# First expert's rows by 0/1 products, early choice for tiles 0 to 2, weights ordered behind the second expert's rows

## What is computed

```python
def hier_moe(t, w_group, b_group, w_expert, b_expert, w_gate, w_up, w_down):
    g_logits = t @ w_group + b_group              # (512, 4)
    g_w, g_idx = lax.top_k(softmax(g_logits), 1)
    e_logits = (t @ w_expert + b_expert).reshape(T, 4, 4)
    e_sel = take_along_axis(e_logits, g_idx)      # the 4 experts of the group
    e_w, e_idx = lax.top_k(softmax(e_sel), 2)
    ...
    for e in range(16):
        hdn = silu(t @ w_gate[e]) * (t @ w_up[e])
        y = y + combine[:, e:e + 1] * (hdn @ w_down[e])
    return y

h = h + hier_moe(rms_norm(h, m_norm[layer]), ...)
```

## Time and profile before

| | us |
|---|---|
| median of 3 runs (1140.46 to 1142.6) | 1140.63 |
| profiled execution | 1143.3 |
| its span, first to last instruction | 1141.5 |
| PE busy | 1078.8 (95%) |
| DVE busy | 508.6 (45%) |
| ACT busy | 282.6 (25%) |
| POOL busy | 265.0 (23%) |
| 16 DMA engines, mean over the span | 248 GB/s |

### The profile page before, as it was taken

One profiled execution on the slowest core, in us unless ns is written; L12 is line 12 of the kernel. 1 busy time (PEld: TensorE's weight loads), 2 busy tenths in 40 slices (PEclk: granted clock), 3 DMA queues, 4 the chain that ended last, 5 costly groups with the idle time before them and its releaser, 6 DMA issues.

```text
span 1141.5 us, 17926 instructions
## 1 busy us (share of the span) xinstructions
PE 1078.8 (95%) x7469; PEld 647.0 (57%) x7469; DVE 508.6 (45%) x939; ACT 282.6 (25%) x461; POOL 265.0 (23%) x373
## 2 busy tenths in 40 slices
PE   6999999999999999996999999999989999999991
PEld 5688887874444433342788877777844444344430
DVE  3465237545533233326422357763355432343317
ACT  4442344320000000004232227763210000000012
POOL 1200012004333443123000013340023344433131
PEclk9899999999999999998999999999989999999996
DMA  9443311248999999998223210004279999999965
GB/s 322 127 146 112 106 38 74 110 186 331 402 422 421 422 423 423 423 418 288 102 75 111 79 69 1 2 1 166 71 263 415 419 421 421 422 423 423 423 230 198
DMA packets 68699, 283.24 MB, mean 248 GB/s; under 512 B 15048, under 2 KB 15216, under 8 KB 44064
## 3 DMA queue, kind: packets, MB, share of 16 engines
q1 hardware_dynamic: 47440, 239.32, 52.3%
q0 software_dynamic: 15232, 38.69, 9.4%
q10 hardware_dynamic: 5968, 4.40, 1.2%
HBM read 259.96 MB, written 22.41 MB: 247 GB/s over the span
## 4 chain that ended last, share of the span: by engine, by line
PE 81%; DVE 6%; DMA 4%; issue 4%; POOL 4%; ACT 1%; SPq 0%; POOLq 0%; DVEq 0%
PE ps L1843 41%; PE ps L1510 11%; PE ps L1512 10%; PE ps L1511 10%; DMA w_f<-in_m_w_up 2%; POOL xn_r L2295 1%; PE ps L1742 1%; DVE h L1384 1%; DMA xn<-output_table,pos 1%; PE ps L1520 1%; PE ps L1971 1%; DVE xn_r L1435 1%; POOL xn_r L2288 1%; PE ps L1654 1%; PE ps L1732 1%
## 5 line engine op out<-in xcount | busy, mean ns | idle before, releaser
L1843 PE MATMUL ps<-raw,s_f 128*32 128x256 f32 (+1 forms) x1536 | 175.8, 455 | 1.3 <-issue 0.7
L1843 PE MATMUL ps<-w_f,s_f 128*32 128x256 f32 (+1 forms) x1536 | 173.0, 451 | 2.6 <-issue 1.8
L1843 PE MATMUL ps<-xT_f,s_f 128*32 128x256 f32 (+1 forms) x1344 | 150.1, 451 | 0.4 <-DMA xT_f<-in_m_w_up 0.4
L1198 DVE TENSOR_TENSOR pad<-pad,ps 128x256 f32<-128x256 f32 x32 | 13.5, 421 | 296.6 <-ACT pad L790 296.6
L1843 PEld LDWEIGHTS ps<-raw,s_f 128*32 128x32 f32 (+1 forms) x1536 | 67.8, 119 | 103.5 <-issue 84.1
L1843 PEld LDWEIGHTS ps<-w_f,s_f 128*32 128x32 f32 (+1 forms) x1536 | 69.1, 119 | 95.4 <-issue 70.5
L1843 PEld LDWEIGHTS ps<-xT_f,s_f 128*32 128x32 f32 (+1 forms) x1344 | 59.7, 119 | 93.0 <-issue 74.0
L939 DVE SCALAR_TENSOR_TENSOR w_lo<-raw,gainT,w_hi 128x512 fp32r<-128x512 f32 x88 | 60.2, 746 | 105.3 <-ACT w_hi L594 105.3
L1208 DVE STREAM_TRANSPOSE s_f<-pad 32x128 f32<-32x128 f32 x256 | 103.0, 403 | 4.1
L1510 PE MATMUL ps<-w_hi,xT_hi 128*128 128x512 f32 x240 | 97.7, 407 | 5.9 <-DVE w_lo L939 2.9
L2252 POOL DMA_DIRECT2D output_table<-pad x60 | 33.7, 566 | 293.0 <-ACT pad L796 282.5
(11 more groups left out here) (299 smaller groups left out, 1470.8 us busy)
## 6 DMA issues: line engine op xcount, KB each, us to landing
raw<-in_m_w_down SPq DMA_DIRECT2D x28, 1024.0 KB
w_f<-in_m_w_down SPq DMA_DIRECT2D x28, 1024.0 KB
xT_f<-in_m_w_gate SPq DMA_DIRECT2D x26, 1024.0 KB
xT_f<-in_m_w_up SPq DMA_DIRECT2D x26, 1024.0 KB
raw<-in_m_w_gate SPq DMA_DIRECT2D x18, 1024.0 KB
raw<-in_m_w_up SPq DMA_DIRECT2D x18, 1024.0 KB
w_f<-in_m_w_gate SPq DMA_DIRECT2D x18, 1024.0 KB
w_f<-in_m_w_up SPq DMA_DIRECT2D x18, 1024.0 KB
```

What stands on the lines that cost most here:

```text
L1198: ve.tensor_tensor(hid2[:, 0:2 * P], sil2[:, 0:2 * P], ps[:, 0, 2 * P:4 * P], ALU.mult)
L1843: ins = te.matmul(ps[rows * n:rows * (n + 1), bank + kind, 0:width // parts], stationary(k, kind), weights(k, parts, n), start=k == 0, sto ...
```

## The change

Three things are changed, in both layers alike.

1. The choice of experts is split by tiles. `select(0, 3)` and the ranks of tiles 0 to 2 are computed while the last tile's projection still runs; `select(3, 4)` and its ranks follow behind its logits. The ranks now lie in PSUM bank 6.
2. Expert 0's rows are no longer gathered. DVE writes for each token and each of the 96 places a 1 where the token takes that place (`first_sel`, float32), and PE multiplies the rows of `xn`, which are on chip, by these lists: 4 tiles x 8 feature blocks = 32 products `first_rows`, whose sum is expert 0's x, already transposed. Expert 1's list is formed by itself (`second_sel`, with `id_parts`, eight products of one column), and the whole-row gather now serves expert 1. The lists for all experts (`lists`), the quarter numbers and expert 1's transposes now stand inside expert 0's kind 0 and kind 1 products (`behind`). The warming products (`kept_warm`) are gone, and expert 1's rows are no longer gathered by quarters.
3. On the SP queue, pair 4 stands ahead of the wait, and the wait is now for expert 1's rows. Pair 6 waits in addition until the products have read `xn`.

The core of the diff:

```diff
@@ load_pair
                 if p == OWN:
                     sp.wait_ge(A["rows_stored"], 16 * NT * (layer + 1))
+                    sp.wait_ge(E["x_tr"], 4 * layer + 2)
@@ step, on the SP queue
+                    load_down(layer, p + 2, e - 1, g)
                     if isinstance(e, int) and e == 1:
-                        sp.wait_ge(E["x_loaded0"], x_loads(layer, 0, -1))
-                    load_down(layer, p + 2, e - 1, g)
+                        sp.wait_ge(E["x_loaded1"], x_loads(layer, 1, -1))
@@ DVE, out_tiles
+            def places_of(sel, e, first, last):
+
+                return tt(sel[:, first:last, :], index_1[:, :].unsqueeze(1).broadcast_to([P, last - first, CAP]),
+                          rank_of_first[:, first:last, e:e + 1].broadcast_to([P, last - first, CAP]), ALU.is_equal)
+
+            def ranks_in(layer, first, last):
+
+                dve.wait_ge(M["ranks_done"], 2 * layer + (1 if first == 0 else 2))
+                link(stt(rank_of_first[:, first:last, :], ps[:, 6, 0:NT * NE].rearrange("p (i e) -> p i e", e=NE)[:, first:last, 0:2], 1.0,
+                         sel_b[:, first:last, 0:2], ALU.add, ALU.mult))
...
-                logits_in(j - 1)
+                link(logits_in(j - 1))
+                select(0, j)
                 add(j, 1)
+                ranks_in(layer, 0, j)
+                places_of(first_sel, 0, 0, j).then_inc(V["places_ready"], 1)
@@ DVE, router
+                select(last, NT)
+                places_of(second_sel, 1, 0, last)
+                ranks_in(layer, last, NT)
+                places_of(first_sel, 0, last, NT).then_inc(V["places_ready"], 1)
+                places_of(second_sel, 1, last, NT).then_inc(V["places_ready"], 1)
...
+                x_half(layer, 0, 0).then_inc(E["x_in"], 1)
...
+                x_half(layer, 0, 1).then_inc(E["x_in"], 1)
+                dve.wait_ge(M["lists_done"], 4 * layer + 1)
+                ve.tensor_copy(token_now[:, 1:2], ps[0:CAP, 2, 2 * P:2 * P + 1]).then_inc(V["tokens_ready"], 1)
@@ PE, out_proj
                 logits(last, range(BK))
+                ranks(layer, range(last))
                 h_transposed_to(last, range(BK, KT))
+                pe.wait_ge(V["places_ready"], 5 * layer + 1)
+                pe.wait_ge(V["xn_ready"], NT * layer + last)
+                first_rows(EARLY[0:4])
                 logits(last, range(BK, KT))
...
+            def first_rows(products):
+
+                for t, k in products:
+                    at = CAP * (k % 4)
+                    ins = te.matmul(ps[:, 4 + k // 4, at:at + CAP], xn[:, t, every(KT, k)], first_sel[:, t, :],
+                                    start=t == 0 and k % 4 == 0, stop=t == NT - 1, skip_group_check=True)
+                return ins
@@ PE, experts
-                x_transposed(E, layer, x_loads(layer, 0, -1))
-                up(I, 0, 0, 0, layer > 0)
-                lists(2 * layer + 2, 7, MAX_OVER)
+                up(I, 0, 0, 0, layer > 0, (lambda: lists(5 * layer + 4, 7, NE), second_rows))
+                lists(5 * layer + 5, 7, MAX_OVER)
@@ PE, router
-                kept_warm(3)
...
+                first_rows(EARLY[4:18])
+                ranks(layer, range(last, NT))
+                first_rows(EARLY[18:20])
+                pe.wait_ge(V["places_ready"], 5 * layer + 2)
+                pe.wait_ge(A["xn_scaled"], layer + 1)
+                first_rows((last, k) for k in range(4)).then_inc(E["x_tr"], 1)
+                first_rows(EARLY[20:])
+                first_rows((last, k) for k in range(4, KT)).then_inc(E["x_tr"], 1)
+                pe.wait_ge(V["places_ready"], 5 * layer + 3)
+                for t in range(NT):
+                    for c in range(2):
+                        ins = te.matmul(ps[0:CAP, 2, 2 * P:2 * P + 1], second_sel[:, t, :], id_parts[:, c, t:t + 1],
+                                        start=t + c == 0, stop=t + c == NT)
+                ins.then_inc(M["lists_done"], 1)
@@ POOL, experts
-                gather(E, token[:, 0:1])
+                gather(token_now[:, 1:2], E["x_loaded1"])
                 pool.wait_ge(V["quads_ready"], layer + 1)
-                gather_quarters(1)
                 gather_quarters(2)
```

More of the change, by code:

```diff
@@ L217, in trunk @@
         gain_rows = pad[0:5 * KT, 13312:13312 + P]
-        free = [6144]
+        free = [11264]
         def scratch(*shape):
@@ L260, in trunk @@
         index = sb("index", [P, CAP])
+        index_1 = sb("index_1", [P, CAP])
+        id_parts = sb("id_parts", [P, 2, NT], BF16)
         parity = sb("parity", [P, 2])
@@ L1790, in every, with ranks @@
                 return slice(k, k + n * (P - 1) + 1, n)
+            EARLY = [(t, k) for f in (0, 1) for t in range(NT - 1) for k in range(4 * f, 4 * f + 4)]
+            def first_rows(products):
[4 more added lines that the diff above has]
+                return ins
+            def ranks(layer, tiles):
+                pe.wait_ge(V["sel_ready"], 2 * layer + (1 if tiles[0] == 0 else 2))
+                for i in tiles:
+                    o = ps[:, 6, NE * i:NE * (i + 1)]
+                    for j in range(i):
+                        te.matmul(o, ones_b[:, :], sel_b[:, j, :], start=j == 0, stop=False)
+                    ins = te.matmul(o, before[:, :], sel_b[:, i, :], start=i == 0, stop=True)
+                if tiles[-1] == NT - 1:
+                    o = ps[:, 6, NE * NT:NE * (NT + 1)]
+                    for j in range(NT):
+                        ins = te.matmul(o, ones_b[:, :], sel_b[:, j, :], start=j == 0, stop=j == NT - 1)
+                ins.then_inc(M["ranks_done"], 1)
             def x_transposed(S, i, loads):
-                pe.wait_ge(S["x_loaded0"], loads)
+                pe.wait_ge(S["x_loaded1" if S is E else "x_loaded0"], loads)
                 for f in (0, 1):
@@ L1846, in column_tiles, with up @@
                     return ins
-                def up(i, p, m, g=0, reuse=True):
-                    pe.wait_ge(E["x_in"], i + 1)
+                def up(i, p, m, g=0, reuse=True, behind=None):
+                    pe.wait_ge(E["x_in"], x_ins(layer, i) - (behind is not None))
                     if reuse:
@@ L1855, in up @@
                                 pe.wait_ge(*pair_of(layer, p + n, g))
+                                if n and behind is not None:
+                                    pe.wait_ge(E["x_in"], x_ins(layer, i))
                             w = pair_slots[slot_of(p + n)]
@@ L1867, in up @@
                                 ins.then_inc(M["blk_used"], 2)
+                            elif behind is not None:
+                                behind[n]()
                 def down(i, p, m, g=0):
@@ L1966, in last_to_tokens @@
                     ins.then_inc(M["last_done"], 1)
-            def kept_warm(n):
-                for _ in range(n):
-                    te.matmul(ps[:, 7, :], ident[:, :], h[:, 0, 0:BN], start=True, stop=True)
             def router(layer):
-                kept_warm(3)
-                pe.wait_ge(V["sel_ready"], layer + 1)
-                for i in range(NT):
-                    o = ps[:, 5, NE * i:NE * (i + 1)]
-                    for j in range(i):
-                        te.matmul(o, ones_b[:, :], sel_b[:, j, :], start=j == 0, stop=False)
-                    te.matmul(o, before[:, :], sel_b[:, i, :], start=i == 0, stop=True)
-                o = ps[:, 5, NE * NT:NE * (NT + 1)]
-                for j in range(NT):
-                    ins = te.matmul(o, ones_b[:, :], sel_b[:, j, :], start=j == 0, stop=j == NT - 1)
-                ins.then_inc(M["ranks_done"], 1)
-                kept_warm(1)
-                lists(2 * layer + 1, 4, NE)
+                last = NT - 1
+                first_rows(EARLY[4:18])
[11 more added lines that the diff above has]
+                                        start=t + c == 0, stop=t + c == NT)
+                ins.then_inc(M["lists_done"], 1)
             out_proj(0)
```

123 lines of the change are left out of this document (66 added, 57 removed).

## The result

The change makes the kernel **slower by 18.2 us**: 1158.85 us median (1157.82 to 1162.17, 4 runs) against 1140.65 us (4 runs of the kernel before on the same chip), ratio 1.016 with a 95% interval of 1.014 to 1.018. The profiled execution took 1162.17 us (span 1160.2), 18.9 more than before; PE's mean granted clock is 0.963 (0.980 before). 1130.7 us was predicted, with 1128.5 to 1132.5 as the forecast's own range and 1136 as the upper end of the range for 8 in 10.

What follows compares the result with a forecast made beforehand. PE was taken as the bound, balanced with the weight stream while experts' weights arrive. Gains of 4.4 (layer 0) and 5.6 (layer 1) less 0.1 gave 9.9 us, from 1140.63 to 1130.7; own range 1128.5 to 1132.5, 8-in-10 range up to 1136.

Steps and rivals of the forecast that it cites:

- Products in place of the gather: Between last logits and first expert: 32 products at 0.215 us each, starting layer 0's first expert 6.15 us earlier.
- The lower bound: Price of the new products: a floor of 0.107 us a record, with 0.1075 taken, 0.215 us a product.
- The upper bound, 0.48: Price per new product from a 256-column row, 0.24 us a record; not expected at 96 columns.
- Rival 3: New products cost the upper price, 0.48 us each, making the kernel slower: 1144 us; chance 0.08.
- its point of 0.39: Price per product, in us, from which products at the upper price use up the whole gain.
- Rival 1, the clock: PE's clock falls in the small products, one more fall in each layer: -3 us, 1133.7 us; chance 0.22.
- What moved into the first expert: Lists, quarter-number records and transposes put 1.75 us into layer 0's first expert; second expert 4.4 us earlier.
- the distance of 1.45 us: Gap between first expert's end and second expert's start, for silu and multiply, taken as kept.
- Weight stream 4.5 earlier: Layer 0's weights: 5.9 us saved by early down pair and one row gather less, minus 1.4 for later resumption.
- Early choice: Selection for tiles 0 to 2 ends by 247.7, hidden behind PE's output projection; last logits about 0.4 us later.
- Sum: Whole kernel: 4.4 for layer 0 plus 5.6 for layer 1 minus 0.1 for small items, 9.9 us.

Runs made afterwards that it cites:

- e2: Kernel before with unread float32 matmuls of varied spacing added behind its last product: 0.235 us a record at every 8th or 4th float, 0.119 at every 2nd.
- e1: Changed kernel with the first expert's products reading their 128 stationary columns side by side (features in another order): 1138.04 us, ratio 0.9982 to the kernel before.
- e10: Changed kernel, spaced reads kept, with 32 idle one-column products added at PE's start to shift its code: 1151.61 us, ratio 1.0088 to the kernel before.
- e4: Kernel before with only the early selection and ranks of tiles 0 to 2: 1139.46 us, ratio 0.9991 [0.9979, 1.0002].
- e6: e1 with 32 idle one-column products added at PE's start to shift its code: 1134.85 us, ratio 0.9956 to the kernel before.
- e7: e1 with 16 idle one-column products added at PE's start to shift its code: 1136.29 us (one run).
- e3: Kernel before with only the first down pair put ahead of the wait for gathered rows on SP: 1148.57 us, ratio 1.0071.

## Why the prediction was wrong

- *Products in place of the gather: the step that failed.* 0.215 us each was taken, 0.48 is right. The lower bound came from side-by-side reads the earlier trace rows, and the spaced ones from transposes; e2 shows that transposes pay next to nothing for spacing and products twice the price. The upper bound, 0.48, came from a row with 256 moving columns, which says nothing of a load; that it met the price is accident.
- *Rival 3* named the right mechanism, though not why, and gave 1144; at 0.48 a product it was past its point of 0.39. It put the second expert of layer 0 at 279.1, and it came at 284.1. Of these 5.0 us 1.7 are a later first expert, 1.3 the clock in it, and 1.7 the late semaphore. It had 0.08 and deserved more, because no row that was read showed a product with a spaced stationary.
- *Rival 1, the clock,* came too, but not as a fall of 3 us at 0.9 to 1.6: some 17 us in each layer. It belongs to the price: the runs at 0.24 a record brought 1.2 GHz in the kernel and in e2, the same run at 0.114 in e1 did not. It cost the first expert 1.3 us (4.96 for 3.65), and 1.7 in layer 1. The forecast priced the rivals one at a time and had no case in which they come together.
- *The Trainium skill's rule* that was set aside ("TensorE: Matmul & The Clock Gate", "Part 3: Packing small matmuls": a load overlaps a running matmul only when the row group differs) was rightly set aside: at 8 apart a record costs 0.235 with 20 or with 96 moving columns (e2), so the load covers the product.
- *What moved into the first expert:* the moved work cost what was said, and PE did not wait for the gather. But the semaphore behind it came 1.8 us late, and the second expert ran 3.0 (layer 0) and 1.5 us (layer 1) longer at 1.2 GHz. The forecast kept the distance of 1.45 us. It had no term for a stall that hangs on the place of PE's code; e10 prices that at 8.3 us.
- *Weight stream 4.5 earlier:* the pair went out at 248.05 as said, but the gather, and the stream behind it, hang on the products: 9.4 later. With the price mended (e1) the gather went out at 258.47, or 260.1 in the times of before, released by the store of the rows; 259.3 was said.
- *Early choice:* hidden, as said, and without an effect on the times alone (e4).
- *Sum:* with both causes out (e6) 1134.85 are reached where 1130.7 was predicted, by the ratio 5.0 of 9.9 us (3.1 to 7.0 by its interval). The profile shows where the rest is. Counted from the last tile's first logits, the second expert comes 4.0 us earlier in layer 0 and 6.5 in layer 1, near what was forecast for PE (4.4, and 6.0 to 6.8). Layer 0 keeps its 4.0 to the end of its experts. Between the layers 2.3 are lost: 1.5 in PE's longer wait (POOL's pause among it) and 0.7 in dense products at 1.2 GHz behind it. The forecast had no term for that. In layer 1 PE waits for weights three times, 1.7 us together, where the kernel before never did: the stream binds, as forecast, but leaves 4.7 and not 5.6. That makes 6.4 (6.6 at the end of the profiles), within the interval. The profiled executions differ by 8.8 because 2.2 lie ahead of the stretch, where PE was granted 0.50 from 50 to 54 us in the kernel before and 1.00 in e6.

## What to carry to other kernels

A duration is only a bound for an instruction with the same operand pattern: check spacing, the transposing form, and which operand moves, and where no row has it, give the upper price a real chance. If an operand must be read with a stride, let it move, or bring it through a transpose. When a gap grows and its releaser is "issue", move the code by a few dozen instructions: it is a cheap test, and a better one than looking whether a transfer of instructions stands near. Before two profiles are compared, see with what lead each comes into the stretch. A product in a wait is worth something by itself if it keeps PE's clock up.

## What the runs showed of the hardware

- A float32 product's record with 128 stationary columns costs 0.11 to 0.12 us at 2.4 GHz with the columns 1 or 2 floats apart (e1, e2), and 0.235 to 0.25 at 4 and 8 apart (e2, the changed kernel), at 8 the same at either clock and with 20 or 96 moving columns. At 1.2 GHz it costs 0.19 to 0.21 side by side and 0.217 at 16 apart. A transpose costs 0.11 to 0.12 at 2.4 GHz at either spacing (e2).
- Runs of records at 0.24 us, with PE and PEld busy without a pause, were granted 1.2 GHz (0.50 from 254 to 266 in the changed kernel, and from 1161 in e2). In e2 the clock came back near the end of the run that stood side by side at 0.193 a record.
- A semaphore of PE came 1.8 us late, once in each layer, and was in time again with PE's code moved by 16 or 32 added products (e6, e7, e10). That PE waited for its own instructions is inferred.
- The store of 512 KB took 2.7 us without and 6.8 us with a weight pair beside it, and what waits for it is late (e3).
